# Expert rows weighted where they are made and summed by an accumulating gather, in an encoder layer's mixture of experts

## The reference, cut to what matters

```python
def hier_moe(h, w_group, b_group, w_erouter, b_erouter, w_gate, w_up, w_down):
    ...
    tv, ti = lax.top_k(el, TOP_K)
    wk = jax.nn.softmax(tv, -1) * pg
    eidx = gidx[:, None] * EXPERTS_PER_GROUP + ti
    combine = jnp.einsum('nk,nke->ne', wk, jax.nn.one_hot(eidx, N_EXPERTS, dtype=jnp.float32)).astype(h.dtype)
    hg = jnp.einsum('nd,edf->nef', hf, w_gate)
    hu = jnp.einsum('nd,edf->nef', hf, w_up)
    act = jax.nn.silu(hg) * hu * combine[:, :, None]
    return jnp.einsum('nef,efd->nd', act, w_down).reshape(B, T, D)
...
    ff = hier_moe(h2, w_group, b_group, w_erouter, b_erouter, w_gate, w_up, w_down)
    x = layer_norm(ALPHA * x + (1 + g2) * ff, ln2_g, ln2_b)
```

## Time and profile before

| | us |
|---|---|
| median of 3 runs (1710.31 to 1710.97) | 1710.92 |
| the profiled execution's own time | 1712.26 |
| its span in the profile | 1710.5 |

### The profile page before, as it was taken

The page is one execution under the profiler, slowest core; times in us unless marked ns, Lnnn a source line. Parts: engine busy times, 40 slices in busy tenths (PEclk is TensorE's granted clock), DMA queues, the critical chain, the costliest instruction groups (busy, mean ns, idle before and its releaser), DMA issues. The chain is left out here.

```text
span 1710.5 us, 26094 instructions
## 1 busy us (share of the span) xinstructions
PE 1443.5 (84%) x7082; PEld 799.1 (47%) x7082; DVE 1400.0 (82%) x3420; ACT 802.2 (47%) x1429; POOL 564.0 (33%) x422
## 2 busy tenths in 40 slices
PE   5977899999999999999997643799999999985654
PEld 1114555665555565555664423455545555541221
DVE  0522999999999999999999317899999999975887
ACT  0411343444434333344443200788888888862232
POOL 0003034444444344444433340121212121205775
PEclk9998899999999999999996665899999999996777
DMA  9953001111111011111011028567894333216774
GB/s 310 397 219 134 13 26 50 50 51 49 49 50 47 15 49 38 50 50 49 37 41 39 25 75 283 191 225 281 315 385 166 123 102 119 109 75 210 229 232 146
DMA packets 90721, 218.28 MB, mean 128 GB/s; under 512 B 8035, under 2 KB 42759, under 8 KB 88592
## 3 DMA queue, kind: packets, MB, share of 16 engines
q1 hardware_dynamic: 65554, 136.25, 22.7%
q0 software_dynamic: 11808, 43.00, 7.9%
q10 hardware_dynamic: 13277, 38.20, 5.8%
HBM read 165.90 MB, written 51.56 MB: 127 GB/s over the span
## 5 line engine op out<-in xcount | busy, mean ns | idle before, releaser
L971 DVE SCALAR_TENSOR_TENSOR y_sum<-uT,w_dw_cols,y_sum 128x128 f32<-128x128 f32 (+1 forms) x1972 | 512.0, 342 | 0.4
L1681 DVE SCALAR_TENSOR_TENSOR w_gate_up_lo<-w_gate_up_ring,w_gate_up_hi 128x2048 f16<-128x2048 f16 x96 | 219.5, 2288 | 24.8 <-ACT w_gate_up_hi L1606 24.4
L1606 ACT ACTIVATE w_gate_up_hi<-w_gate_up_ring 128x2048 f16 x96 | 182.8, 1906 | 59.0 <-SPq L1564 40.1
L1106 PE MATMUL bank<-w_in_hi,hT_hi 128*128 128x512 f16 (+3 forms) x544 | 195.2, 359 | 1.1 <-DVE hT_lo L1088 1.1
L1106 PE MATMUL bank<-w_in_lo,hT_hi 128*128 128x512 f16 (+3 forms) x544 | 194.9, 358 | 0.0
L1106 PE MATMUL bank<-w_in_hi,hT_lo 128*128 128x512 f16 (+3 forms) x544 | 194.6, 358 | 0.0
L1724 PE MATMUL ps_up<-w_gate_up_hi,slot_rowsT_hi 128*128 128x512 f16 x384 | 147.0, 383 | 19.0 <-DVE slot_rowsT_lo L1706 18.2
L1587 POOL COPY slot_index<-slot_token 128x1 int32 (+1 forms) x48 | 44.9, 935 | 351.7 <-PE eturn L1745 308.5
L1724 PE MATMUL ps_up<-w_gate_up_lo,slot_rowsT_hi 128*128 128x512 f16 x384 | 146.6, 382 | 0.0
L1724 PE MATMUL ps_up<-w_gate_up_hi,slot_rowsT_lo 128*128 128x512 f16 x384 | 146.4, 381 | 0.0
L733 POOL TENSOR_TENSOR y_small<-y_small,mhalf 128x1 f32<-128x1 f32 (+1 forms) x17 | 9.4, 550 | 407.2 <-DVE y_small L1002 407.2
(11 more groups left out here) (255 smaller groups left out, 3098.9 us busy)
## 6 DMA issues: line engine op xcount, KB each, us to landing
w_ada_ring<-in_w_ada SPq DMA_DIRECT2D x12, 2048.0 KB, 13.7
expert_rows<-out_rows ACTq DMA_DIRECT2D x48, 512.0 KB, 2.6
w_gate_up_ring<-in_w_gate SPq DMA_DIRECT2D x16, 1024.0 KB, 9.2
w_gate_up_ring<-in_w_up SPq DMA_DIRECT2D x16, 1024.0 KB, 12.7
w_down_ring<-in_w_down SPq DMA_DIRECT2D x16, 1024.0 KB, 12.9
x_h<-in_x_prompt SPq DMA_DIRECT2D x16, 512.0 KB
x_res<-in_x_prompt SPq DMA_DIRECT2D x16, 512.0 KB, 3.3
hidden<-h SPq DMA_DIRECT2D x16, 512.0 KB, 2.6
```

Of the source, the lines that this page charges most:

```text
L971: dve.scalar_tensor_tensor(total, u, w, y_sum[:, c, :n], ALU.mult, ALU.add).then_inc(taps_done, 1)
L1106: mm = pe.matmul(out, x[xp][:, k, :n], w[wp][:, k, cols], start=(k == 0 and wp == xp), stop=(k == KD - 1 and xp == 1))
L1606: act.activation(gate_up_parts[0][:, at, k:k + KD // 2, :, :].rearrange("p k a n -> p (k a n)"), w_gate_up[:, bass.ds(b, 1), k:k + KD // 2 ...
L1681: dve.scalar_tensor_tensor(flat[1], w_gate_up[:, bass.ds(b, 1), k, :, :].rearrange("p b k a n -> p (b k a n)"), W_SCALE, flat[0], ALU.mult ...
```

## The change

Three blocks are edited.

In `route` a table `slot_weight` is made beside `slot_token`: `at_tile` gets a second set of 48 columns with the weight of the pair, so PE's 34 products have 96 columns instead of 48. The one-hots are no longer made pair by pair in rings, but for all pairs at once in four groups (9 and 8 tiles for each choice s), with tensor_tensor operations over whole groups. The weights of the 64 unused rows of tile 0 are set to zero.

In `experts` ACT multiplies a slot tile's column of `slot_weight` by the constant scale into a small buffer, waits for it, and uses that column as the scale of the two copies from `ps_out`. So the rows in `expert_rows` carry their weights already.

`finish` is written anew, without a hardware loop. A token's two rows are added by the DMA: the first pick writes a buffer, the second is an indirect gather with `compute_op=ALU.add` into the same buffer, after waiting for the first. There are seven pick buffers, four of `x1`, three of `y` and four of the sums in PSUM. First picks are issued six tiles ahead, second ones three. The gate row is multiplied in place, in halves. POOL keeps only the picks and the power; the offset row is added by DVE.

```diff
@@ route @@
-        at_offset = sb("at_offset", [P, SLOT_RING, P])
-        at_tile = sb("at_tile", [P, SLOT_RING, SLOT_TILES])
+        at_offset = sb("at_offset", [P, 2, T, P])
+        at_tile = sb("at_tile", [P, 2, T, 2, SLOT_TILES])
...
-                for n in range(NPAIR):
-                    pe.wait_ge(onehots_ready, 2 * n + 2)
-                    pe.matmul(ps_slot[:, 0:SLOT_TILES], at_offset[:, n % SLOT_RING, :], at_tile[:, n % SLOT_RING, :],
-                              start=(n == 0), stop=(n == NPAIR - 1)).then_inc(slots_done, 1)
+                for n, (s, ts) in enumerate(PARTS):
+                    pe.wait_ge(onehots_ready, n + 1)
+                    for t in range(ts.start, ts.stop):
+                        mm = pe.matmul(ps_slot[:, 0:2 * SLOT_TILES], at_offset[:, s, t, :], at_tile[:, s, t].rearrange("p a j -> p (a j)"),
+                                       start=(n == 0 and t == 0), stop=(n == len(PARTS) - 1 and t == T - 1))
+                mm.then_inc(slots_done, 1)
...
+                    done(dve.tensor_tensor(at_offset[:, s, ts, :], per_column(column[:], P), per_pair(part[:, 1, s, ts], P), ALU.is_equal))
+                    done(dve.tensor_tensor(at_tile[:, s, ts, 0, :], per_column(tile_no[:], SLOT_TILES),
+                                           per_pair(part[:, 0, s, ts], SLOT_TILES), ALU.is_equal))
+                    done(dve.tensor_tensor(at_tile[:, s, ts, 1, :], at_tile[:, s, ts, 0, :],
+                                           per_pair(K["pair_weight"][:, ts, s], SLOT_TILES), ALU.mult))
+                    dve.tensor_tensor(at_tile[:, s, ts, 0, :], at_tile[:, s, ts, 0, :],
+                                      per_pair(token_id[:, ts], SLOT_TILES), ALU.mult).then_inc(onehots_ready, 1)
+                dve.wait_ge(slots_done, 1)
+                done(dve.tensor_copy(K["slot_weight"][:], ps_slot[:, SLOT_TILES:2 * SLOT_TILES]))
@@ experts, ACT @@
+                            act.wait_ge(out_ready, count(2, j, -2))
+                        act.activation(weight[:, c:c + 1], K["slot_weight"][:, tile_at(j)], ACT.Copy, scale=1.0 / W_SCALE).then_inc(weight_ready, 1)
+                        act.wait_ge(weight_ready, count(1, j, 1))
                         for h in range(2):
                             act.wait_ge(down_done, count(2, j, h + 1))
-                            act.activation(out_rows[:, c, h * 512:(h + 1) * 512], ps_out[h][:], ACT.Copy, scale=1.0 / W_SCALE).then_inc(out_ready, 1)
+                            act.activation(out_rows[:, c, h * 512:(h + 1) * 512], ps_out[h][:], ACT.Copy, scale=weight[:, c:c + 1]).then_inc(out_ready, 1)
@@ finish @@
+PICK_RING, X1_RING, Y_RING, SUM_RING = 7, 4, 3, 4
...
+                for t in range(2, X1_RING):
+                    load_x1(t)
+                for t in range(TILES):
+                    if t + X1_RING < TILES:
+                        load_x1(t + X1_RING)
...
+                def pick(t, s):
+                    b = t % PICK_RING
+                    offset = bass.IndirectOffsetOnAxis(ap=K["pair_slot"][:, t, s:s + 1], axis=0)
+                    if s == 0:
+                        if t >= PICK_RING:
+                            pool.wait_ge(added, 2 * (t - PICK_RING) + 2)
+                        pool.indirect_dma_start(out=picked[:, b, :], out_offset=None, in_=expert_rows[:, :],
+                                                in_offset=offset).then_inc(first_picked[b], 16)
+                    else:
+                        pool.wait_ge(first_picked[b], 16 * (t // PICK_RING + 1))
+                        pool.indirect_dma_start(out=picked[:, b, :], out_offset=None, in_=expert_rows[:, :],
+                                                in_offset=offset, compute_op=ALU.add).then_inc(both_picked[b], 16)
...
+                FIRST_AHEAD, BOTH_AHEAD = PICK_RING - 1, PICK_RING - 4
+                for t in range(FIRST_AHEAD):
+                    pick(t, 0)
+                for t in range(BOTH_AHEAD):
+                    pick(t, 1)
+                for t in range(TILES):
+                    power(t)
+                    if t + BOTH_AHEAD < TILES:
+                        pick(t + BOTH_AHEAD, 1)
+                    if t + FIRST_AHEAD < TILES:
+                        pick(t + FIRST_AHEAD, 0)
...
+                gate(0)
+                for t in range(TILES + 1):
+                    if t < TILES:
+                        statistics(t)
+                    if t + 1 < TILES:
+                        gate(t + 1)
+                    if t < TILES:
+                        shift(t)
+                    if t >= 1:
+                        gain(t - 1)
```

230 lines of the change are left out of this document (92 added, 138 removed).

## The result

| | before | after |
|---|---|---|
| median us | 1710.95 (1710.31 to 1716.12, 4 runs) | 1682.06 (1681.39 to 1683.45, 4 runs) |
| span of the profiled execution | 1710.5 | 1681.7 |
| slot table: expert_end written to slot_token written | 15.5 | 14.9 |
| expert stage: slot_token to first pick | 479.2 | 489.7 |
| last stage: first pick to the end | 167.7 | 128.1 |

The changed kernel takes 0.9821 of the time before (95% interval 0.9807 to 0.9834): 28.9 us less, where I had forecast 13. The sign and the two large terms, a gain at the end and a loss in the expert stage, came out; the gain was 40 us instead of 25.5.

A forecast was written before the change was run, and what follows sets the result against it. It took a ring through POOL's offset addition, with DVE's shift stuck beside it, to bound the last stage's tile. Last stage -25.5, slot table +4, experts +9 gave -12.5 us: 1698 us, range 1679 to 1726.

The forecast's parts named there:

- the two large terms: Last stage ends 25.5 us earlier; expert stage grows by 9 us.
- The tile of 6.9 us: Last stage: each token tile takes 6.9 us, between 6.3 and 7.5 (PE at the half clock), against 9.09 before.
- DVE's sum: Last stage: DVE's work for a tile, statistics, gate, shift, gain and offset, comes to 5.85 us.
- the 0.45 for the power: Last stage: DVE waits some 0.45 us a tile for POOL's power, slowed beside the gate, making 6.3 us.
- rival (a): Last stage: the DMA queues become the bound, 18.5 us gained and 13 paid, 1705 us; chance 0.20.
- Rival (b): Last stage: the accumulating pick costs much more than two plain ones, 1733 us on average; chance 0.15.
- k: Price of an accumulating pick in plain picks; the forecast took twice a plain pick's packets, 3.5 us.
- The fill and the drain: Last stage: fill costs 10 us more (8 to 12), first gate near 1560; drain 14.6 us against 22.
- The slot table: Router's slot table stage grows by 4 us, between 1.3 and 8.
- The expert stage: ACT's added work, 0.4 us a tile (0.25 to 0.63), costs the stage 9 us, bounds 0 and 30.
- Rival (c): Expert stage: ACT's addition counts in full on every tile, 30 us, giving 1719 us; chance 0.10.
- (d): Picks at the plain price, tile at 6.3 us, small additions stay hidden: 1679 us; chance 0.09.

## Why the prediction was wrong in size

Right in sign and inside its range, but 16 us off. By profiled spans the change is -28.8: the stages ahead +1.0, slot table -0.7, experts +10.5, last stage -39.6.

**The tile of 6.9 us is the step that failed**: 16 x 6.9 = 110.4 in the sum, 97.8 measured, 12.6 of the 16 us. I took PE at the half clock, because the earlier trace rows shows 0.74 for the stage before. In after the granted clock from 1590 on is 0.91, and halving PE's work gave 1.4 us. An average clock of the old stage was no property of the new one; why it is higher no run isolates. What sets the tile instead is the queues, with DVE and its waits for PE close behind: 6.28 us where the share is 1.03, and 5.6 with plain second picks. DVE's sum was near (5.85 in the text, 5.41 measured: the gate 1.20 and not 1.4, the shift 0.07 and not 0.2, gain and offset 2.39 and not 2.5), and the 0.45 for the power was right for a whole gate and wrong for the gate in halves, which is in the diff.

**The queues were rival (a), with the right mechanism and the wrong price.** At the rates of the earlier trace rows, share 0.64, a plain pick costs 1.74 us and an accumulating one was put at two of them, 3.5. In the new last stage they cost 1.47 and 2.4 with full queues (1.51 and 2.6 over the whole stage). The 34 picks took 69.6 us, not 89. Why a plain pick is cheaper in the new stage is open. How full the queues are does not explain it, for the kernel before with only the offset moved (share 0.85, q0 from 1570 to 1650) shows

```profile
q0 software_dynamic: 3138, 11.43, 51.8%
```

which is 1.90 us a pick, more than at 0.64. I had the 386 GB/s window of the earlier trace rows beside it and used it as an argument only, not in the sum. The Trainium skill (Collectives: The Full Stack, "Why ReduceScatter is half of AllGather") gives 1.93 as the measured ratio of AllGather's bandwidth to that of ReduceScatter, whose add needs two source reads; for a gather of 4 KB rows the runs here show 1.6 to 1.7. Rival (b), k over 2, is excluded.

**The fill and the drain were right**: first gate 16.7 us after the stage's start (18.2 in the sum), drain 14.2 (14.6).

**The slot table** is the second term that was mis-sized: +4 in the sum, -0.7 measured. DVE's operations took what the form of L1462 says (1152 elements 1.36 us), but PE's last 16 passes took 2.02 instead of 3.4, and the price of 96 columns, up to 0.08 a pass, did not show. The window of the table has a granted clock of 0.75, against 0.50 before, and 1.00 from 1058 on. That the clock is the cause was argued from these rows; no run isolates it. The range, 1.3 to 8, left the outcome out.

**The expert stage** was right: +9 in the sum, +10.5 measured, 11.2 when the addition is taken away. The addition of 0.49 a tile lay in the bounds 0.25 to 0.63, and about half of it was paid, at the wait for the second split. Rival (c), paid in full, falls; so does the hope of (d) that it stays hidden.

**What the sum never priced** was the depth of the ring. With five buffers and shorter leads the whole gain of 29 us was gone (the last stage 34.5 longer).

## What to carry to other kernels

When a tiny operation lasts exactly as long as a long one on the engine beside it, moving that one long operation may be most of the gain; try it alone before a redesign. Price transfers in bulk with a margin, for the same 512 KB pick took 1.47 to 1.90 us of packet time in different kernels here, and ask of each ring buffer which engine issues into it and what that engine waits for. A per-row factor belongs on an operation that already has a scalar operand, on the engine that is not in the ring, and its copy behind whatever must not wait.

## What the runs showed of the hardware that I had not expected

- An accumulating gather costs 2.4 us of packet time for 512 KB in 4 KB rows, 1.64 plain ones, with the queues full, and 2.6 or 1.7 over the whole stage.
- Its issue takes POOL 1.53 to 1.59 us in the fill, where DVE is idle, a plain one 0.94 to 0.95. Later the place in the row counts for more: in the same place the accumulating one takes 1.97 at the median and a plain one 2.05, while the first picks take 0.99 and 0.94.
- In windows of 55 to 75 us a share of 1.03 to 1.04 of 16 engines moved 325 to 334 GB/s with accumulating picks, and 1.00 moved 380 with plain ones.
- A DVE operation on SBUF in two halves leaves a seam: POOL's power took 0.93 us beside it, 1.47 beside the same work in one operation, and ended 0.42 behind the DVE operation in both.
- An ACT copy of 128x512 from PSUM takes 584 ns with a constant scale and 683 with a column; DVE's scalar_tensor_tensor of 128x256 from SBUF and PSUM takes 421 and 481.
